# Two attentions whose first pair is loaded a phase earlier, and a third gate/up chunk with its work in another order

## The chip, the cores and the metric

The kernel runs on one core of one Trainium2 chip. A core has TensorE (matmuls; PE in the rows, with PEld for its weight loads), VectorE (DVE), ScalarE (ACT), GpSimd (POOL) and SyncE (SP), which here only issues transfers. The engines run their own instruction lists and meet at semaphores. The metric is the device time of one execution in microseconds (us), as the median of several runs.

## The reference

One inference step of a two-layer encoder on 1024 prompt tokens and 32 sample tokens (N = 1056 columns), D = 1024, all float32. Each layer is a mixer and a SwiGLU feed-forward part:

```python
# layer 0 mixer: sparse attention A (8 heads, top-k keys) beside a gated linear recurrence B
# layer 1 mixer: chunked attention C (16 heads, own chunk and 8 before)
logits = q @ k.T * DH ** -0.5 + bias;  p = softmax(logits);  out = p @ v
x = x + gate * (mix @ w_out)
h = modulate(x, norm_ffn)
x = x + gate2 * ((silu(h @ w_gate) * (h @ w_up)) @ w_down)      # D_FF = 2816
```

A matmul keeps float32 accuracy by splitting each operand into an upper half (fp32r) and a rest, and making three passes: upper by upper, rest by upper, upper by rest.

## The kernel before

The program is a row of phases, with a barrier of all engines between two of them: `front_phase` (projections of layer 0, the choice of the keys), `attention_phase` "pa" (A), the recurrence, `trunk_phase` 0, `attention_phase` "pc" (C), `trunk_phase` 1. There is no scheduler: each engine's list is written out by hand, and instructions wait on semaphores.

**The end of the front phase and of a trunk phase.** TensorE makes the last projections, ScalarE copies each to a stage and stores it to z (q and k by feature) or zt (v by token). VectorE chooses keys at the front's end and SyncE stores that mask.

**An attention phase.** Heads go in pairs g, each over 8 row tiles, unit u = (g, i). `loads(g)` on SyncE issues q, k, bias and v of a pair, two pairs ahead in two buffers; `loads(0)` and `loads(1)` are the first things in the phase. For a unit TensorE makes the scores (L2284) once q and k are in; in A GpSimd first adds bias and mask (L2255), in C it masks two corners of the bias once a pair (L2249, L2250); VectorE adds the result to the scores (L2420); ScalarE takes the exponentials (L2523); TensorE turns them (L2297) and, three units behind the scores, multiplies by v (L2312).

**The gate/up part of a trunk phase.** There are KF = 22 chunks of 128 features. The first two (f = 0, 1, "the pair") are made plainly, in four rounds of products (`pair_products`, phases 0 to 3: M1, M2 for the left half of the columns, B12, M3 for the right), each round of four: f = 0 gate, f = 0 up, f = 1 gate, f = 1 up. A product is 24 matmuls of 264 columns. From the third chunk on (f = 2, weights of unit `SEVEN`) a chunk takes seven products of a fast 2x2 scheme, in the order M1, M2, M6, M5, M7, M3, M4 (`up_products`). Its inputs for M6, M5, M7, M4 are differences of quarters `full[0]` to `full[3]` of the activations:

- ScalarE shifts the quarters (`shift_tile`, L843), 4 tiles each;
- GpSimd makes the differences in `full[0]`, `full[1]`, `full[3]` (L584, L588, L591), VectorE then the one in `full[2]` (L1332);
- ScalarE casts each to its upper half (`upper`, L867), VectorE subtracts for the rest (`lower`, L1135), in the order M6, M5, M7, M4.

In between stand the results of the pair: `pair_silu(f, right)` on ScalarE (L871) reads the gate product out of PSUM, `pair_product(f, right)` on VectorE (L1142) multiplies by the up product, `pair_store` on ScalarE's queue stores it. A PSUM bank is free only after that, so TensorE waits: in `pair_products` phase 2 for `pair_gate[f]` >= 1 and `pair_value[f]` >= 1, in `up_products(2)` before M1, M2, M6 and M5 for `pair_gate[0]`, `pair_value[0]`, `pair_gate[1]`, `pair_value[1]` >= 2. Before M7 it waits for ScalarE's copy of M1 (`keep_m1`, L900), before M3 for VectorE's first sum of the chunk (`sum_gate_left`, L1153).

The weights of a chunk are split into a ring of six slots: an upper half (cast on GpSimd, L550, or on ScalarE, L889) and a rest (GpSimd, L552); four combinations of the quarters of the weights (L561 to L567, `combine`) are on GpSimd too. `by_act` says which casts are ScalarE's: all of the chunks from `SEVEN` on, but not the first six slots of `SEVEN` itself.

## Time and profile before

| | |
|---|---|
| median of 3 runs | 3113.55 us (3110.88 to 3113.63) |
| the profiled execution, its own time | 3111.68 us |
| its span, first to last instruction | 3109.8 us |
| TensorE busy | 2917.9 us (94%) |
| VectorE, ScalarE, GpSimd busy | 1653.1, 951.2, 1321.6 us |
| mean granted clock of TensorE | 0.971 |
| phase starts: A, C | 579.96, 2006.14 us |

The granted clock is a share of full speed: 1.00 is 2.4 GHz, 0.50 is 1.2 GHz. A row of a timeline gives start, duration, engine and line; a bracket at its end gives how long the engine stood idle before it and what released it. SPq and ACTq are the queues that issue transfers.

### The profile page before, as it was taken

What the parts mean: (1) busy time and instruction counts of PE and PEld (TensorE: products, weight loads), DVE (VectorE), ACT (ScalarE), POOL (GpSimd) and SP (SyncE); (2) the same over time, 40 slices, a digit from 0 to 9 for tenths busy, and PEclk for the clock granted to TensorE, in tenths of its full rate; (3) what the DMA queues carried; (4) which work ended last, traced back from release to release, by engine and by line L of the source; (5) the groups of instructions that cost most, each with busy time, mean ns of one, the idle gap of its engine ahead of it and who ended that gap; (6) DMA issues with size and microseconds to landing.
All of it is one profiled execution on the core that took longest, in us unless ns stands there. A gap on an engine that the chain in (4) does not pass through costs nothing. (4 is left out here: it accounts for less than half of the span.)

```text
span 3109.8 us, 60214 instructions
## 1 busy us (share of the span) xinstructions
PE 2917.9 (94%) x25097; PEld 2716.4 (87%) x25097; DVE 1653.1 (53%) x2959; ACT 951.2 (31%) x1984; POOL 1321.6 (42%) x1082
## 2 busy tenths in 40 slices
PE   7999999886789899999999999899889999999998
PEld 5859999664679899999999999766689999999998
DVE  6399999564646644445346400055536644444345
ACT  3341211354433433332101311165524333332001
POOL 2112212373533877776334222100114877775334
PEclk8999999998889999999999999999989999999999
DMA  5816763633241122223321232352121122224222
GB/s 211 256 61 228 235 212 106 180 108 110 99 164 55 49 83 83 82 70 133 102 83 62 81 103 74 95 191 86 64 85 45 66 83 80 71 78 153 83 74 72
DMA packets 160465, 338.82 MB, mean 109 GB/s; under 512 B 21033, under 2 KB 94529, under 8 KB 152193
## 3 DMA queue, kind: packets, MB, share of 16 engines
q1 hardware_dynamic: 119856, 281.64, 27.0%
q10 hardware_dynamic: 40336, 53.31, 4.8%
q8 instruction: 200, 3.28, 0.4%
q14 instruction: 73, 0.59, 0.1%
HBM read 268.30 MB, written 79.49 MB: 112 GB/s over the span
## 5 line engine op out<-in xcount | busy, mean ns | idle before, releaser
L108 PE MATMUL tr_acc<-tr_quad_hi,ah_ring_hi 128*128 128x264 f32 x2432 | 696.3, 286 | 18.8 <-DVE tr_kept L1142 13.2
L110 PE MATMUL tr_acc<-tr_quad_hi,ah_ring_lo 128*128 128x264 f32 x2432 | 694.7, 286 | 0.0
L109 PE MATMUL tr_acc<-tr_quad_lo,ah_ring_hi 128*128 128x264 f32 x2432 | 692.4, 285 | 0.0
L552 POOL TENSOR_TENSOR ah_ring_lo<-ah_raw,ah_ring_hi 128x512 fp32r<-128x512 f32 (+1 forms) x402 | 553.9, 1383 | 183.0 <-ACT ah_ring_hi L889 169.2
L108 PEld LDWEIGHTS tr_acc<-tr_quad_hi,ah_ring_hi 128*128 128x128 f32 x2432 | 461.0, 190 | 19.7 <-DVE tr_kept L1142 13.6
L109 PEld LDWEIGHTS tr_acc<-tr_quad_lo,ah_ring_hi 128*128 128x128 f32 x2432 | 461.2, 190 | 0.1
L110 PEld LDWEIGHTS tr_acc<-tr_quad_hi,ah_ring_lo 128*128 128x128 f32 x2432 | 460.4, 189 | 0.0
L550 POOL CAST ah_ring_hi<-ah_raw 128x512 fp32r<-128x512 f32 (+1 forms) x172 | 113.4, 659 | 592.3 <-PE tr_acc L110 527.2
L108 PE MATMUL tr_acc<-tr_part_hi,ah_ring_hi 128*128 128x352 f32 x1038 | 335.5, 323 | 2.0 <-DVE tr_kept L1191 2.0
L109 PE MATMUL tr_acc<-tr_part_lo,ah_ring_hi 128*128 128x352 f32 x1038 | 332.8, 321 | 0.0
L110 PE MATMUL tr_acc<-tr_part_hi,ah_ring_lo 128*128 128x352 f32 x1038 | 332.5, 320 | 0.0
L1228 DVE SCALAR_TENSOR_TENSOR x<-tr_acc,mod,x 128x352 f32<-128x352 f32 (+2 forms) x384 | 166.8, 487 | 265.6 <-PE tr_acc L110 265.6
L2420 DVE CUSTOM_DVE_ANT_0 pc_prob<-pc_dots,pc_bias 128x640 f32<-128x640 f32 (+4 forms) x128 | 83.2, 652 | 348.0 <-POOL pc_bias L2250 268.2
L1412 DVE TENSOR_SCALAR_CACHE_REDUCE f_q<-score,choose_trial 128x384 bf16<-128x384 f32 (+6 forms) x224 | 242.1, 1146 | 1.1
L889 ACT ACTIVATE ah_ring_hi<-ah_raw 128x512 fp32r<-128x512 f32 x230 | 143.5, 626 | 248.1 <-POOL ah_raw L567 177.5
L108 PE MATMUL f_acc<-h_hi,f_w_hi 128*128 128x352 f32 x600 | 202.3, 337 | 6.8 <-DVE h_lo L2016 6.8
L108 PEld LDWEIGHTS tr_acc<-tr_part_hi,ah_ring_hi 128*128 128x128 f32 x1038 | 194.8, 188 | 2.5 <-DVE tr_kept L1191 2.4
L109 PEld LDWEIGHTS tr_acc<-tr_part_lo,ah_ring_hi 128*128 128x128 f32 x1038 | 195.0, 188 | 0.1
L110 PEld LDWEIGHTS tr_acc<-tr_part_hi,ah_ring_lo 128*128 128x128 f32 x1038 | 194.6, 187 | 0.0
L1714 POOL CAST f_w_hi<-f_raw 128x2048 fp32r<-128x2048 f32 (+1 forms) x15 | 28.4, 1895 | 389.9 <-DMA f_raw<-in_w_dram 197.4
L110 PE MATMUL f_acc<-h_hi,f_w_lo 128*128 128x352 f32 x600 | 193.6, 323 | 0.0
L109 PE MATMUL f_acc<-h_lo,f_w_hi 128*128 128x352 f32 x600 | 193.5, 322 | 0.0
(399 smaller groups left out, 6484.6 us busy)
## 6 DMA issues: line engine op xcount, KB each, us to landing
f_ada_w<-in_w_ada_dram SPq DMA_DIRECT2D x48, 1024.0 KB, 5.5
scratch_inner<-tr_kept ACTq DMA_DIRECT2D x88, 264.0 KB, 2.4
tr_staged<-scratch_inner SPq DMA_DIRECT2D x44, 528.0 KB, 4.0
ah_raw<-in_w_gate_dram SPq DMA_DIRECT2D x44, 512.0 KB, 3.5
ah_raw<-in_w_up_dram SPq DMA_DIRECT2D x44, 512.0 KB, 4.5
ah_raw<-in_w_down_dram SPq DMA_DIRECT2D x64, 256.0 KB, 3.1
f_raw<-in_w_dram SPq DMA_DIRECT2D x24, 512.0 KB, 7.4
out_z_dram<-f_stage ACTq DMA_DIRECT2D x60, 176.0 KB, 1.9
```

The lines of the kernel that those rows point to most:

```text
L108: pe.matmul(out, w_hi, hi, start=start, stop=False)
L109: pe.matmul(out, w_hi, lo, start=False, stop=False)
L110: return pe.matmul(out, w_lo, hi, start=False, stop=stop)
L550: pool.tensor_copy(hi[:, 0:width], own).then_inc(w_hi, 1)
L552: pool.tensor_tensor(lo[:, 0:width], own, hi[:, 0:width].bitcast(F32), ALU.subtract).then_inc(w_ready, 1)
L889: act.activation(slot(u, to)[0], factor_of(u, to), ACT.Copy).then_inc(act_hi, 1)
L1228: done = dve.scalar_tensor_tensor(out=x[:, k, lo:hi], in0=pair[s % 3][:, a, lo - THIRD * t:hi - THIRD * t], scalar=gate_ffn[:, k, of:of + ...
L1412: last = dve.tensor_scalar(marks[n % 2][0:p, 0:width], score[0:p, at:at + width], bound(p, j), 0.0, compare, ALU.add, accum_out=count[0:p, ...
L1714: pool.tensor_copy(w[b].hi[:, 0:n], raw[b][:, 0:n]).then_inc(w_hi, 1)
L2420: dve.tensor_tensor_reduce(prob[2 * (u % 3) + hd][:, 0:n], dots[hd][:, at_dots(u):at_dots(u) + n], add, -DH ** -0.5, 3.0e38, ALU.add, ALU. ...
```

## The change

It has two parts.

**First pair loaded early.** A class `FirstPair` holds q, k and bias of pair 0 at a place that the phase before no longer needs: in the front phase the two raw weight buffers, in trunk 0 the quarters 11 to 13 of the arena. SyncE issues the three loads there at the end of its list in the phase before (in the front ahead of the mask's store), behind waits for the last weight split and for the stores of z; it waits for their landing before the phase ends. The attention phase lays its other tiles around that place, issues only v for pair 0, and TensorE and GpSimd wait for no load at pair 0.

**Third chunk.** `pair_silu(1, 0)` moves ahead of M3's casts, `pair_silu(0, 1)` and `pair_silu(1, 1)` and both right `pair_product`s move forward; half of the differences in `full[1]` and `full[3]` go from GpSimd to VectorE; the six remaining casts of `SEVEN` go to ScalarE; GpSimd splits slot 2 of every chunk before its fourth combination, and ScalarE casts it after the third.

```diff
-        self.by_act = [SEVEN <= u < DOWN_FIRST and i >= self.slot_no[SEVEN, 6] for i, (u, n) in enumerate(self.slots)]
+        self.by_act = [SEVEN <= u < DOWN_FIRST for i, (u, n) in enumerate(self.slots)]
...
+        def differences(eng, k):
+            if k < KH // 2:
+                eng.wait_ge(combo, KH + KH // 2 + k + 1)
+            else:
+                eng.wait_ge(combo_upper, k + 1)
...
@@ trunk, SyncE
+            if ahead:
+                for r in range(3):
+                    sp.wait_ge(stored[r], 16 * 2 * 5)
+                ahead.loads(sp)
+                ahead.done(sp)
...
@@ combine(u), GpSimd
                 pool.wait_ge(combined, 4 * f + 3)
+                split(u, 2, r11)
                 pool.tensor_tensor(r12, r12, r11, ALU.subtract).then_inc(combined, 1)
...
-            for k in range(KH):
+            for k in range(KH // 2):
                 pool.wait_ge(shifted, 2 * KH + k + 1)
                 pool.wait_ge(combo, k + 1)
                 pool.tensor_tensor(full[1][:, k], full[3][:, k], full[1][:, k], ALU.subtract).then_inc(combo, 1)
-            for k in range(KH):
+            for k in range(KH // 2):
                 pool.wait_ge(combo, KH + k + 1)
                 pool.tensor_tensor(full[3][:, k], full[3][:, k], full[0][:, k], ALU.subtract).then_inc(combo, 1)
...
@@ cast, ScalarE
-                    act.wait_ge(combined, 4 * (u - SEVEN) + 4)
+                    act.wait_ge(combined, 4 * (u - SEVEN) + (3 if to == 2 else 4))
...
@@ the third chunk, ScalarE
             pair_silu(0, 0)
+            pair_silu(1, 0)
             for k in range(KH):
                 upper(M3, k)
...
+            pair_store(1, 0)
+            pair_silu(0, 1)
+            cast_slot(plan.slot_no[SEVEN, 0])
+            cast_slot(plan.slot_no[SEVEN, 1])
             for k in range(KH):
                 upper(M6, k)
-            pair_store(1, 0)
             for k in range(KH):
                 upper(M5, k)
-            pair_silu(0, 1)
+            pair_store(0, 1)
+            pair_silu(1, 1)
+            for n in range(2, 6):
+                cast_slot(plan.slot_no[SEVEN, n])
...
@@ the third chunk, VectorE
             pair_product(1, 0)
+            for k in range(KH // 2, KH):
+                dve.wait_ge(shifted, 2 * KH + k + 1)
+                dve.wait_ge(combo, k + 1)
+                dve.tensor_tensor(full[1][:, k], full[3][:, k], full[1][:, k], ALU.subtract).then_inc(combo_upper, 1)
+            for k in range(KH // 2, KH):
+                dve.wait_ge(combo_upper, k - KH // 2 + 1)
+                dve.tensor_tensor(full[3][:, k], full[3][:, k], full[0][:, k], ALU.subtract).then_inc(combo_upper, 1)
             for k in range(KH):
                 lower(M6, k)
+            pair_product(0, 1)
             for k in range(KH):
-                dve.wait_ge(combo, 2 * KH + k + 1)
+                differences(dve, k)
                 dve.wait_ge(shifted, 3 * KH + k + 1)
                 dve.tensor_tensor(full[2][:, k], full[2][:, k], full[3][:, k], ALU.subtract).then_inc(combo4, 1)
+            pair_product(1, 1)
             for k in range(KH):
                 lower(M5, k)
-            pair_product(0, 1)
             for k in range(KH):
                 lower(M7, k)
-            pair_product(1, 1)
...
@@ the front phase, SyncE
+            sp.wait_ge(lines_out, 48)
+            sp.wait_ge(w_ready, len(units))
+            projected = store_no[plan.last_step[len(units) - 3]] + 1
+            for r in range(3):
+                sp.wait_ge(stored[r], 16 * len(range(r, projected, 3)))
+            ahead.loads(sp)
             store_mask(sp)
-            sp.wait_ge(lines_out, 48)
+            ahead.done(sp)
...
+class FirstPair:
+    def loads(self, sp):
+        q, k, bias = self.sources
+        sp.dma_start(self.bias[:], bias).then_inc(self.landed, 16)
+        sp.dma_start(self.q[:], q).then_inc(self.landed, 16)
+        sp.dma_start(self.k[:], k).then_inc(self.landed, 16)
+    def done(self, sp):
+        sp.wait_ge(self.landed, 48)
...
@@ attention, SyncE, loads(g); the waits of GpSimd and TensorE likewise
-                sp.dma_start(q[b][:], z[q0 + g][:, 0:T]).then_inc(qk_in[b], 16)
-                sp.dma_start(k[b][:], z[k0 + g][:, 0:T]).then_inc(qk_in[b], 16)
+                if g:
+                    sp.dma_start(q[b][:], z[q0 + g][:, 0:T]).then_inc(qk_in[b], 16)
+                    sp.dma_start(k[b][:], z[k0 + g][:, 0:T]).then_inc(qk_in[b], 16)
```

How instructions stand on the engines is seen in the orders of the two programs (names with numbers are tiles: before, `tr_full_11354` to `tr_full_11357` are `full[0]` to `full[3]`, `tr_kept_11394` and `tr_kept_11396` the right values of the pair, `tr_kept_11397` the left value of f = 1; after, the same tiles are `tr_full_11361` to `tr_full_11364`, `tr_kept_11401`, `tr_kept_11403` and `tr_kept_11404`).

ScalarE at the third chunk of trunk 0, before, from the last shift:

```order
L843 ACTIVATE tr_full_11356<-tr_full_11356,mod 128x528 x4
L867 ACTIVATE tr_quad_hi<-tr_full_11357 128x528 x4
L876 DMA scratch_inner<-tr_kept_11397 128x528
L867 ACTIVATE tr_quad_hi<-tr_full_11354 128x528 x4
L871 ACTIVATE tr_kept_11394<-tr_acc 128x528
L867 ACTIVATE tr_quad_hi<-tr_full_11355 128x528 x4
L876 DMA scratch_inner<-tr_kept_11394 128x528
L871 ACTIVATE tr_kept_11396<-tr_acc 128x528
L867 ACTIVATE tr_quad_hi<-tr_full_11356 128x528 x4
L876 DMA scratch_inner<-tr_kept_11396 128x528
```

And in the changed kernel, from the same shift:

```order
L860 ACTIVATE tr_full_11363<-tr_full_11363,mod 128x528 x4
L896 DMA scratch_inner<-tr_kept_11404 128x528
L891 ACTIVATE tr_kept_11401<-tr_acc 128x528
L911 ACTIVATE ah_ring_hi<-ah_raw_9100 128x512 x2
L887 ACTIVATE tr_quad_hi<-tr_full_11364 128x528 x4
L887 ACTIVATE tr_quad_hi<-tr_full_11361 128x528 x4
L896 DMA scratch_inner<-tr_kept_11401 128x528
L891 ACTIVATE tr_kept_11403<-tr_acc 128x528
L911 ACTIVATE ah_ring_hi<-ah_raw_9100 128x512
L911 ACTIVATE ah_ring_hi<-tr_w_sum_11398 128x512
L911 ACTIVATE ah_ring_hi<-ah_raw_9100 128x512 x2
L887 ACTIVATE tr_quad_hi<-tr_full_11362 128x528 x4
```

Both right SiLUs now stand ahead of M7's casts, the first ahead of M6's too, and six weight casts are new.

VectorE at the same place, before, from the left value product of f = 1:

```order
L1142 TENSOR_TENSOR tr_kept_11397<-tr_kept_11397,tr_acc 128x528
L1135 TENSOR_TENSOR tr_quad_lo<-tr_full_11357,tr_quad_hi 128x528 x4
L1332 TENSOR_TENSOR tr_full_11356<-tr_full_11356,tr_full_11357 128x528 x4
L1135 TENSOR_TENSOR tr_quad_lo<-tr_full_11354,tr_quad_hi 128x528 x4
L1142 TENSOR_TENSOR tr_kept_11394<-tr_kept_11394,tr_acc 128x528
L1135 TENSOR_TENSOR tr_quad_lo<-tr_full_11355,tr_quad_hi 128x528 x4
L1142 TENSOR_TENSOR tr_kept_11396<-tr_kept_11396,tr_acc 128x528
L1135 TENSOR_TENSOR tr_quad_lo<-tr_full_11356,tr_quad_hi 128x528 x4
L1153 TENSOR_TENSOR tr_kept_11397<-tr_kept_11393,tr_acc 128x528
```

And in the changed kernel:

```order
L1168 TENSOR_TENSOR tr_kept_11404<-tr_kept_11404,tr_acc 128x528
L1356 TENSOR_TENSOR tr_full_11362<-tr_full_11364,tr_full_11362 128x528 x2
L1359 TENSOR_TENSOR tr_full_11364<-tr_full_11364,tr_full_11361 128x528 x2
L1161 TENSOR_TENSOR tr_quad_lo<-tr_full_11364,tr_quad_hi 128x528 x4
L1168 TENSOR_TENSOR tr_kept_11401<-tr_kept_11401,tr_acc 128x528
L1366 TENSOR_TENSOR tr_full_11363<-tr_full_11363,tr_full_11364 128x528 x4
L1168 TENSOR_TENSOR tr_kept_11403<-tr_kept_11403,tr_acc 128x528
L1161 TENSOR_TENSOR tr_quad_lo<-tr_full_11361,tr_quad_hi 128x528 x4
L1161 TENSOR_TENSOR tr_quad_lo<-tr_full_11362,tr_quad_hi 128x528 x4
L1161 TENSOR_TENSOR tr_quad_lo<-tr_full_11363,tr_quad_hi 128x528 x4
L1179 TENSOR_TENSOR tr_kept_11404<-tr_kept_11400,tr_acc 128x528
```

Four differences are new on VectorE, the right value product of f = 0 stands after four operations of M6 instead of after twelve, that of f = 1 after eight instead of sixteen.

SyncE's queue at the border of the front phase and attention A, before:

```order
L1612 DMA f_raw<-in_wt_dram 128x4x256 x4
L1469 DMA scratch_mask_s<-score 32x2080
L87 UNCONDITIONAL_BRANCH
L2161 UNCONDITIONAL_BRANCH
L2167 DMA pa_q<-out_z_dram 128x1024
L2168 DMA pa_k<-out_z_dram 128x1024
L2171 DMA pa_bias<-scratch_skew_a 128x2x1024
L2174 DMA pa_v<-out_zt_dram 128x8x128
L2167 DMA pa_q<-out_z_dram 128x1024
L2168 DMA pa_k<-out_z_dram 128x1024
```

And in the changed kernel:

```order
L1648 DMA f_raw<-in_wt_dram 128x4x256 x4
L2125 DMA pa_bias_53<-scratch_skew_a 128x2x1024
L2126 DMA pa_q_54<-out_z_dram 128x1024
L2127 DMA pa_k_55<-out_z_dram 128x1024
L1502 DMA scratch_mask_s<-score 32x2080
L88 UNCONDITIONAL_BRANCH
L2232 UNCONDITIONAL_BRANCH
L2247 DMA pa_v<-out_zt_dram 128x8x128
L2239 DMA pa_q<-out_z_dram 128x1024
L2240 DMA pa_k<-out_z_dram 128x1024
```

Bias, q and k of pair 0 went from behind the border to ahead of the mask's store; v is now the first load of the phase. At the border of trunk 0 and C the same three stand last in the trunk.

## Rows read from the trace of the kernel before

**Rows 1.** TensorE's waits, whole span: line, releaser: us in total, times, longest.
```profile
PE pa_dots L2284 <- DMA pa_k<-out_z_dram: 8.4, 1, 8.4
PE pc_dots L2284 <- DMA pc_k<-out_z_dram: 9.0, 1, 9.0
```

**Rows 2.** Timeline, start of attention A: start us, duration us, engine, line, operation.
```profile
579.96 0.37 SPq L2167 DMA_DIRECT2D pa_q<-out_z_dram  x1
...
587.74 5.37 POOL L2255 TENSOR_TENSOR pa_extra<-pa_bias,score 128x128 f32<-128x128 f32 x7 [7.32 <-DMA pa_bias<-scratch_skew_a]
...
588.35 0.29 DVE L2420 CUSTOM_DVE_ANT_0 pa_prob<-pa_dots,pa_extra 128x128 f32<-128x128 f32 x1 [19.92 <-POOL pa_extra L2255]
...
594.35 0.70 PE L2312 MATMUL pa_out<-pa_probT,pa_v 128*64 128x128 f32 x4
```

**Rows 3.** Tile pa_v, 570 to 700 us: issue to landing of its four loads.
```profile
DMA to landing us min/median/max: 3.9/8.3/13.5
```

**Rows 4.** Timeline, start of attention C.
```profile
2006.14 0.34 SPq L2167 DMA_DIRECT2D pc_q<-out_z_dram  x1
...
2013.07 0.20 POOL L2249 MEMSET pc_bias<- 64x128 f32 x1 [6.25 <-DMA pc_bias<-scratch_skew_c]
...
2013.67 0.29 DVE L2420 CUSTOM_DVE_ANT_0 pc_prob<-pc_dots,pc_bias 128x128 f32<-128x128 f32 x1 [268.16 <-POOL pc_bias L2250]
```

**Rows 5.** Timeline of SyncE's queue, 500 to 579 us, all of it.
```profile
567.67 0.34 SPq L1469 DMA_DIRECT2D scratch_mask_s<-score  x1
```

**Rows 6.** Windows: busy us (x) of PE, PEld, DVE, ACT, POOL; granted clock; DMA.
```profile
584.00:586.00 2.00, 0.95 (x6) 0.93 (x8) 0.00 (x0) 0.00 (x0) 0.00 (x0) 0.50 1.04 426
1046.00:1048.00 2.00, 1.40 (x6) 1.41 (x7) 2.00 (x3) 1.70 (x4) 2.00 (x2) 0.50 0.29 113
1052.00:1054.00 2.00, 2.00 (x17) 2.00 (x16) 2.00 (x3) 1.13 (x2) 1.92 (x3) 0.89 0.35 135
1100.00:1150.00 50.00, 50.00 (x414) 50.00 (x413) 26.65 (x25) 15.98 (x27) 38.89 (x29) 1.00 0.19 65
```

**Rows 7.** Timeline of TensorE, 1014 to 2434 us: its stops at the third chunk.
```profile
1018.62 0.59 PE L108 MATMUL tr_acc<-tr_quad_hi,ah_ring_hi 128*128 128x264 f32 x1 [2.85 <-ACT tr_kept L871]
...
1046.60 0.59 PE L108 MATMUL tr_acc<-tr_quad_hi,ah_ring_hi 128*128 128x264 f32 x1 [5.90 <-DVE tr_kept L1142]
...
2401.74 0.39 PE L108 MATMUL tr_acc<-tr_quad_hi,ah_ring_hi 128*128 128x264 f32 x1 [2.77 <-ACT tr_kept L871]
...
2429.76 0.59 PE L108 MATMUL tr_acc<-tr_quad_hi,ah_ring_hi 128*128 128x264 f32 x1 [7.27 <-DVE tr_kept L1142]
```

**Rows 8.** Timeline of ScalarE, 990 to 1060 us.
```profile
1018.46 5.87 ACT L843 ACTIVATE tr_full<-tr_full,mod 128x496 f32<-128x496 f32 x12
...
1034.74 0.59 ACT L871 ACTIVATE tr_kept<-tr_acc 128x528 f32<-128x528 f32 x1
...
1052.47 0.61 ACT L900 ACTIVATE tr_kept<-tr_acc 128x528 f32<-128x528 f32 x1 [2.78 <-PE tr_acc L110]
```

**Rows 9.** Timeline of GpSimd, 990 to 1090 us.
```profile
1015.71 5.10 POOL L584 TENSOR_TENSOR tr_full<-tr_full,tr_full 128x528 f32<-128x528 f32 x4 [25.90 <-ACT tr_full L843]
...
1025.89 6.12 POOL L591 TENSOR_TENSOR tr_full<-tr_full,tr_full 128x528 f32<-128x528 f32 x4
...
1086.00 1.29 POOL L552 TENSOR_TENSOR ah_ring_lo<-ah_raw,ah_ring_hi 128x512 fp32r<-128x512 f32 x1 [0.87 <-ACT ah_ring_hi L889]
```

**Rows 10.** Timeline of VectorE, 990 to 1060 us.
```profile
1027.94 1.14 DVE L1135 TENSOR_TENSOR tr_quad_lo<-tr_full,tr_quad_hi 128x528 fp32r<-128x528 f32 x1 [8.57 <-ACT tr_quad_hi L867]
...
1045.85 0.69 DVE L1142 TENSOR_TENSOR tr_kept<-tr_kept,tr_acc 128x528 f32<-128x528 f32 x1
...
1057.48 0.69 DVE L1153 TENSOR_TENSOR tr_kept<-tr_kept,tr_acc 128x528 f32<-128x528 f32 x1
```

**Rows 11.** Lines L1332 and L1135: ns of one, min/median/max.
```profile
L1332 DVE TENSOR_TENSOR tr_full<-tr_full,tr_full x8: 1108/1797/1810, 1033.5 to 2421.2; 128x528 f32<-128x528 f32 x8
L1135 DVE TENSOR_TENSOR tr_quad_lo<-tr_full,tr_quad_hi x4: 884/1368/1604, 1027.9 to 1032.7; 128x528 fp32r<-128x528 f32 x4
```

107 lines of the change are left out of this document (67 added, 40 removed).

## Prediction

> **What bounds the kernel now.** I read the windows first. In 1100 to 1150 us, the middle of the gate/up chunks, TensorE is busy 50.00 of 50 us at granted clock 1.00, while GpSimd has 38.89 and VectorE 26.65 [rows 6]: TensorE's queue is the bound there, and time is only to be had where it stops. The list of TensorE's waits for transfers shows two such stops, 8.4 us at the start of attention A and 9.0 us at the start of C [rows 1]; its timeline shows four at the third chunk, 2.85 and 5.90 us in trunk 0, 2.77 and 7.27 us in trunk 1 [rows 7]. The change aims at these six. The windows show a second price of a stop: after the one that ends at 1046.60 the clock stands at 0.50, and is 0.89 over 1052 to 1054, so it is back at about 1052.4 [rows 6]. A spell of 5.8 us at half speed loses 2.9 us.
>
> **First pair early, attention A.** The phase starts at 579.96, its first real step is VectorE's at 588.35, which waits for GpSimd's sum at 587.74, which waits 7.32 us for the bias [rows 2]. With bias, q and k in place GpSimd begins after its two short memsets: the sum was ready to go at 587.74 - 7.32 = 580.42, so VectorE's first step comes at 588.35 - 7.32 = 581.03. TensorE's scores need some 0.6 us from 579.96 and are no later. Gain 7.3 us. **What is late next:** v of pair 0, used first at 594.35 [rows 2], now 587.0. It was issued fourth and is now issued first, at 580.0; landings of this tile took 3.9, 8.3 in the median and 13.5 us at most [rows 3]. The 3.9 and the 8.3 give 583.9 and 588.3, the 13.5 gives 593.5; with nothing queued ahead of it I take the low half, 584 to 587, and a loss of nothing to 0.1: 7.2 us stay. The second pair is needed eight units later and issued a little earlier than before.
>
> **Attention C.** The same: start 2006.14, the mask on the bias at 2013.07 after 6.25 us of waiting for it, VectorE at 2013.67 [rows 4]. That makes 6.25 us, and the three loads that are no longer ahead of v's spare the queue 0.1: 6.4 us, from a start at 2007.3.
>
> **What the early loads cost.** In the front phase SyncE's queue issues nothing between 500 and 579 us but the mask's store at 567.67 [rows 5]. The last weight split ends long before that, so the three loads go out in the idle part, some 40 us ahead of the end, and the 13.5 us of the slowest landing seen fits three times. Without that cover they would cost what they cost now. In the trunk they follow the last weights and wait for z stores made long ago. I charge nothing for both, and up to 1 us in the range.
>
> **Third chunk, what moves.** One product is 24 matmuls; 50.00/414 us each [rows 6] gives 2.90 us. All in trunk 0's times:
> - *First stop.* TensorE stopped at 1018.62 - 2.85 = 1015.77 for the SiLU of f = 1 [rows 7], which stood behind M3's casts and four shifts. It now follows the SiLU of f = 0 and is done by about 1008.5; the value product beside it is VectorE's at 1015.7. The stop goes. Six products (the rest of phase 2, phase 3) then end at 1015.77 + 6 x 2.90 = 1033.2, M1 of f = 2 at 1036.1, M2 could follow at once.
> - *Differences.* GpSimd makes the first four from 1015.71 in 5.10 us, and four more, beside VectorE, in 6.12 [rows 9]. Now it has four left after 1020.8 where it had eight: at 1.28 to 1.53 each they end at 1025.9 to 1027.0. VectorE does its four from 1020.6, at 0.88 alone to 1.80 beside GpSimd [rows 11], by 1024.1 to 1027.8. ScalarE reaches M6's casts at 1024.5 (when phase 3's first product is done, which the SiLU of f = 0 needs) + 3 x 0.6 = 1026.3. So VectorE starts on M6's rests at about 1027.1 instead of 1027.94 [rows 10].
> - *Second stop.* TensorE waited for the value product at 1045.85 [rows 7, 10]. VectorE took 5.6 us for M6's four rests (1027.94 to 1033.5) [rows 10, 11]; the product of 0.69 us now follows them, and is done at 1033.4. M2 starts at 1036.1 without waiting, M6 at 1039.0 (its SiLU is done by 1034.6, its weights by 1037.7), and ends at 1041.9.
> - *What is late next* is VectorE's chain, which has not become shorter. After 1033.4 eight operations stand at (1045.85 - 1033.5)/8 = 1.54 us: differences to 1039.6, the second value product to 1040.3, M5's rests one by one to about 1045.8. TensorE, at M5 from 1042, goes at their pace and ends M5 near 1047.7. M7 needs ScalarE's copy of M1, which stands behind M7's and M4's casts as it did (1052.47 before) [rows 8], now about 1049.3. M3 needs the first sum, 1057.48 before [rows 10], behind eight more rests. GpSimd, rid of six casts, runs out of work near 1045; at 0.88 the eight take 7.0, and the sum is done at 1053.6. At the old rate, (1057.48 - 1046.54)/8 less the one product = 1.28, it is 1056.8.
> - *Balance.* M3 and M4 end 5.8 us after that sum: 1059.4, at the old rate 1062.6. Before, six products followed 1046.60, with the half-speed spell: 1046.60 + 17.4 + 2.9 = 1066.9. Gain 7.5 or 4.3 us. Trunk 1 differs by 1383.2: the end was 2429.76 + 20.3 = 2450.1 against 2442.6 or 2445.8, the same 7.5 or 4.3. New short stops at M5, M7 and M3 (2.7, 1.6 and 1.1 us) can bring a half-speed spell of their own. I take 6 in each trunk: near the fast end, less half a spell. Together 12.
>
> **Steady chunks.** Slot 2 is split ahead of the fourth combination; slots 3 to 6 come no earlier and no later but for a second round trip to ScalarE. Such a wait is 0.87 us [rows 9]; a chunk of 20.3 us leaves GpSimd 11.1/50 of it idle [rows 6], 4.5 us. It hides. Cost nothing; without that cover 0.87 a chunk.
>
> **A rule of the Trainium skill against this step.** L1332's operations, with two inputs in SBUF, took 1.797 us in the median beside GpSimd, where the shortest like it took 0.884 [rows 11]. "SBUF — State Buffer", Who interferes with whom, says that such a VectorE instruction and a GpSimd one that reads SBUF lock each other out for the whole instruction. By the rows' rates the shared differences end at 1027.0. Taken as a strict lock, four of 1.28 and four of 0.88 stand in one line from 1020.8 and end at 1029.4, 2.4 us later. The rows lie between: 1.54 each on VectorE over 12 us in which GpSimd too was never idle. I go by them.
>
> **The sum.** 7.2 + 6.4 + 12 = 25.6 us. 3111.68 - 25.6 = 3086.1. The profiled execution stands 1.9 us under the median of the three runs, but the lowest is below it, so I add half: 3087.
>
> **The rivals.**
> - *VectorE's chain stays the bound at its old pace and a half-speed spell comes in both trunks.* For it: the chain has 20 operations as before, and the new short stops. Per trunk 4.3 - 2.9 = 1.4. Gain 16.4: 3096.
> - *The differences take turns at SBUF.* For it the long rows of L1332. The chain is 2.4 us later in each trunk: gain 20.8: 3092. (This is the rule's case above.)
> - *The wait passes to v.* If it takes the 13.5 us in each attention, 6.4 of the gain go each time: 12.8 less, 3099. Against it: nothing is queued ahead.
> - *The clock.* At 584 to 586 it is 0.50 [rows 6], since TensorE had stopped. A stop of 3.5 us instead of 8.4 may spare one spell of 2.9 in each attention: 5.8 more, 3081.
> - *Slower.* The second round trip delays the rest of slot 3 in each of 20 chunks in two trunks, 0.87 each if GpSimd's queue has no slack: +35 against -25.6 makes 3121. It decides from the point where the idle 4.5 us of a chunk are used up; the windows speak against it.
> - *Nothing.* The engines' starts move, but another wait of the same length stands behind each: 3112.
>
> **How the numbers follow.** Forecast 0.62 (3080 to 3092 its own range), chain and clock 0.15, turns at SBUF 0.08, v 0.05, clock kept 0.04, slower 0.03, nothing 0.03. 3079 to 3096 leaves out v, slower, nothing and the tails. A measurement tells 0.2% (6.2 us) from no change. Faster by more: 0.62 + 0.15 + 0.08 + 0.05 + 0.04 = 0.94; within 0.03; slower 0.03.
>
> **What would show it.** Right: no transfer among TensorE's waits at either attention; VectorE's first step 1.1 to 1.2 us after the phase's start; the value product of f = 0 right before 1033.5 less what came off earlier, no stop of TensorE at M2; in their place short stops at M5, M7 and M3, released by VectorE and ScalarE. Wrong: a wait of TensorE for v; GpSimd named as releaser in the steady chunks; a first sum of the chunk no earlier than before by 1 us; the phase borders moved later by the early loads.

## The result, and the profile after

The changed kernel takes 3084.07 us in the median of four runs (3080.31 to 3085.46), the kernel before 3113.59 (3110.88 to 3119.29). The ratio is 0.9897 with a 95% interval of 0.988 to 0.9915: faster by 29.5 us by the medians. The forecast was 3087, with a range of 3079 to 3096. The profiled execution took 3085.13 us, its span is 3083.3, 26.5 less than before; the prediction's sum of 25.6 us was made for such a pair.

| | before | after |
|---|---|---|
| span of the profiled execution | 3109.8 | 3083.3 |
| TensorE busy | 2917.9 | 2912.0 |
| mean granted clock | 0.971 | 0.976 |
| A: start of the phase to the last value product | 145.1 | 139.0 |
| trunk 0: first to last product of the gate/up part | 470.4 | 463.5 |
| C: start of the phase to the last value product | 236.6 | 230.2 |
| trunk 1: first to last product of the gate/up part | 472.0 | 465.2 |

The last four lines are differences of the first and the last start that the views of one tile give (the value products that read v; the products that read the tile of quarters; for a phase's start SyncE's first load in it). They give 6.2 (before rounding), 6.9, 6.4 and 6.8, together 26.3 us. In this pair of profiles these four places are the whole change, and the rest of the program takes as long as before (from trunk 0's last gate/up product to the start of C, where the early loads of C are issued, 551.9 us against 552.0). Another profile of the changed kernel, after_again below, differs elsewhere by 3.4 us.

**The attentions.** The timelines of the profile after, at the start of A, against [rows 2]:

```profile
533.25 0.37 SPq L2125 DMA_DIRECT2D pa_bias<-scratch_skew_a  x1
...
534.18 0.43 SPq L2127 DMA_DIRECT2D pa_k<-out_z_dram  x1
...
580.45 0.40 SPq L2247 DMA_DIRECT2D pa_v<-out_zt_dram  x1
...
580.98 22.75 POOL L2328 TENSOR_TENSOR pa_extra<-pa_bias,score 128x128 f32<-128x128 f32 x18
...
581.59 0.29 DVE L2493 CUSTOM_DVE_ANT_0 pa_prob<-pa_dots,pa_extra 128x128 f32<-128x128 f32 x1 [13.38 <-POOL pa_extra L2328]
...
580.48 0.93 PE L2357 MATMUL pa_dots<-pa_k,pa_q 64*128 64x128 f32 x8 [3.36 <-PEq L80]
```

and of C, against [rows 4]:

```profile
1993.44 0.38 SPq L2247 DMA_DIRECT2D pc_v<-out_zt_dram  x1
...
1994.18 0.20 POOL L2322 MEMSET pc_bias<- 64x128 f32 x1
...
1994.78 0.29 DVE L2493 CUSTOM_DVE_ANT_0 pc_prob<-pc_dots,pc_bias 128x128 f32<-128x128 f32 x1 [261.67 <-POOL pc_bias L2323]
```

The three loads of A are issued at 533 us, 47 us ahead of the phase, those of C at 1890.9 to 1891.9, 101 us ahead. In the phase v is the first load, VectorE's first step comes 1.1 us after the start in A and 1.3 in C, where it was 8.4 and 7.5. TensorE waits for no transfer at either place; the 3.36 us in front of its row are the border itself.

**The third chunk.** TensorE's stops there, in trunk 0 (the first four rows) and trunk 1, against [rows 7]:

```profile
1037.26 0.36 PE L109 MATMUL tr_acc<-tr_quad_hi,ah_ring_hi 128*128 128x264 f32 x1 [0.90 <-issue]
...
1039.48 0.39 PE L109 MATMUL tr_acc<-tr_quad_hi,ah_ring_hi 128*128 128x264 f32 x1 [0.90 <-DVE tr_quad_lo L1161]
...
1047.23 0.39 PE L109 MATMUL tr_acc<-tr_quad_hi,ah_ring_hi 128*128 128x264 f32 x1 [1.01 <-DVE tr_kept L1179]
...
1062.79 0.39 PE L109 MATMUL tr_acc<-tr_quad_hi,ah_ring_hi 128*128 128x264 f32 x1 [0.72 <-DVE tr_kept L1224]
...
2412.46 0.39 PE L109 MATMUL tr_acc<-tr_quad_hi,ah_ring_hi 128*128 128x264 f32 x1 [1.27 <-ACT tr_kept L922]
...
2416.84 0.39 PE L109 MATMUL tr_acc<-tr_quad_hi,ah_ring_hi 128*128 128x264 f32 x1 [1.20 <-DVE tr_kept L1179]
```

The stops of 2.85 and 5.90 us, 2.77 and 7.27 in trunk 1, are gone. In their place are stops of about 1 us: two in M5 (0.90 each), one at M7 (1.27 in trunk 1), one at M3 (1.01 and 1.20), and one of 0.72 in the chunk behind, which the prediction's sum did not have. The first of the two in M5 names no releaser, but M5 reads the weights of slot 3, and GpSimd's rest of that slot ends at 1037.15, right before it; M5's second stop is for VectorE's rests. VectorE and GpSimd there, against [rows 9, 10]:

```profile
1014.84 2.67 DVE L1356 TENSOR_TENSOR tr_full<-tr_full,tr_full 128x528 f32<-128x528 f32 x2 [4.17 <-ACT tr_full L860]
...
1017.42 3.59 DVE L1359 TENSOR_TENSOR tr_full<-tr_full,tr_full 128x528 f32<-128x528 f32 x2
...
1021.16 6.76 DVE L1161 TENSOR_TENSOR tr_quad_lo<-tr_full,tr_quad_hi 128x528 fp32r<-128x528 f32 x4
...
1027.84 0.69 DVE L1168 TENSOR_TENSOR tr_kept<-tr_kept,tr_acc 128x528 f32<-128x528 f32 x1
...
1028.45 5.22 DVE L1366 TENSOR_TENSOR tr_full<-tr_full,tr_full 128x528 f32<-128x528 f32 x4
...
1034.21 12.35 DVE L1161 TENSOR_TENSOR tr_quad_lo<-tr_full,tr_quad_hi 128x528 fp32r<-128x528 f32 x12
...
1046.49 0.69 DVE L1179 TENSOR_TENSOR tr_kept<-tr_kept,tr_acc 128x528 f32<-128x528 f32 x1
...
1018.65 3.54 POOL L608 TENSOR_TENSOR tr_full<-tr_full,tr_full 128x528 f32<-128x528 f32 x2
...
1035.70 1.45 POOL L568 TENSOR_TENSOR ah_ring_lo<-tr_w_sum,ah_ring_hi 128x512 fp32r<-128x512 f32 x1 [0.87 <-ACT ah_ring_hi L911]
...
1048.52 3.01 POOL L568 TENSOR_TENSOR ah_ring_lo<-ah_raw,ah_ring_hi 128x512 fp32r<-128x512 f32 x2 [3.76 <-ACT ah_ring_hi L911]
```

VectorE has no gap of more than 0.2 us from 1014.84 to the first sum, which is done at 1047.18; M3 starts at 1047.23. GpSimd ends its differences at 1022.2, and stands idle for 3.76 us ahead of 1048.52. The windows, against [rows 6]:

```profile
584.00:586.00 2.00, 2.00 (x6) 0.65 (x6) 1.21 (x5) 1.59 (x6) 2.00 (x3) 0.53 1.04 414
586.00:588.00 2.00, 1.24 (x10) 0.62 (x8) 1.53 (x5) 1.36 (x4) 2.00 (x3) 1.00 1.02 403
1040.00:1042.00 2.00, 2.00 (x11) 2.00 (x10) 2.00 (x3) 2.00 (x5) 0.58 (x1) 0.50 0.35 135
1042.00:1044.00 2.00, 2.00 (x12) 1.71 (x12) 2.00 (x4) 1.31 (x3) 0.61 (x1) 0.69 0.00 0
1100.00:1150.00 50.00, 50.00 (x414) 50.00 (x413) 19.77 (x21) 15.40 (x26) 37.54 (x28) 1.00 0.26 89
```

In A the clock is back at full by 586 us. In trunk 0 a short spell at half speed follows the stops in M5; trunk 1 shows none (2402 to 2422 us at 1.00). The spell cost nothing here: from M5's start to M7's it is 5.59 us in trunk 0 (1037.26 to 1042.85) and 5.60 in trunk 1 (2406.86 to 2412.46), since M7 waits for ScalarE's copy of M1 either way, and the stop of 1.27 us of trunk 1 is what the spell fills in trunk 0. bounds_later below has the stop and not the spell in trunk 0, and the trunk takes 463.6 us, as long as here. The steady chunks are as they were: TensorE busy 50.00 of 50 us with the same 414 matmuls.

### The profile page after: what moved, and what is told of

It is laid out like the page before. It is cut to its first block and busy times, and to the rows that moved or that the text cites. A ratio compares the mean times of both kernels' runs of the same rounds, so it can differ in the third digit from the quotient of the medians.

```text
span 3083.3 us, 60268 instructions
## 1 busy us (share of the span) xinstructions
PE 2912.0 (94%) x25097; PEld 2709.4 (88%) x25097; DVE 1617.8 (52%) x2967; ACT 955.1 (31%) x1996; POOL 1300.1 (42%) x1062
## 5 line engine op out<-in xcount | busy, mean ns | idle before, releaser
L566 POOL CAST ah_ring_hi<-ah_raw 128x512 fp32r<-128x512 f32 (+1 forms) x162 | 103.9, 641 | 593.4 <-PE tr_acc L111 527.2
```

What stands on the lines that cost most here:

```text
L566: pool.tensor_copy(hi[:, 0:width], own).then_inc(w_hi, 1)
```

## The experiments

Every variant computes the whole reference. Its time is the median of four or five executions, and its ratio is taken to executions of the kernel before beside it. A single program spreads over 3 to 11 us between executions, so differences under 3 us are read from the phases of the profiles, which repeat within 0.3 us in the trunks. There is one profile behind each row. The table gives for each kernel the four stretches of the table above.

| kernel | time | ratio to before, interval | A | trunk 0 | C | trunk 1 |
|---|---|---|---|---|---|---|
| before | 3111.8 to 3113.6 | | 145.1 | 470.4 | 236.6 | 472.0 |
| changed | 3084.07 | 0.9897, 0.988 to 0.9915 | 139.0 | 463.5 | 230.2 | 465.2 |
| after_again | 3083.02 | 0.9904, 0.9888 to 0.9921 | 139.0 | 463.5 | 230.1 | 465.3 |
| early_only | 3097.71 | 0.9959, 0.9946 to 0.9972 | 141.0 | 470.6 | 230.4 | 471.7 |
| third_only | 3098.98 | 0.9955, 0.9942 to 0.9967 | 146.5 | 463.5 | 236.6 | 465.2 |
| silu_back | 3085.70 | 0.9915, 0.9902 to 0.9929 | 139.1 | 466.2 | 230.5 | 466.6 |
| value_back | 3099.95 | 0.9959, 0.9947 to 0.9972 | 137.9 | 470.9 | 230.7 | 472.5 |
| diffs_back | 3091.12 | 0.993, 0.9917 to 0.9942 | 139.4 | 466.8 | 230.3 | 468.6 |
| casts_back | 3089.46 | 0.993, 0.9917 to 0.9942 | 141.1 | 466.7 | 230.4 | 469.7 |
| split_back | 3080.71 | 0.9897, 0.9882 to 0.9912 | 138.9 | 462.2 | 229.1 | 464.0 |
| sum_first | 3086.71 | 0.9922, 0.9907 to 0.9936 | 137.4 | 466.1 | 230.5 | 465.2 |
| sums_first | 3083.01 | 0.9903, 0.9888 to 0.9918 | 137.9 | 462.3 | 229.2 | 464.1 |
| bounds_later | 3081.02 | 0.9895, 0.988 to 0.9909 | 135.2 | 463.6 | 230.2 | 465.2 |
| best | 3080.57 | 0.9889, 0.9874 to 0.9904 | 135.8 | 462.3 | 230.7 | 464.1 |

### The two parts alone

**early_only** is the kernel before with all hunks of the early loads and none of the third chunk; **third_only** is the reverse.

> The kernel before with the early loads of both attentions alone; the third chunk as before. In the profile of the changed kernel the steps of A stand 7.3 us earlier from the fourth unit on and 5.7 us earlier after the stop of TensorE near 664 us, behind which the clock is low there and was not before; C gains 6.6. Theory: the two parts of the change add up, this one gives 12.3 (A 5.7, C 6.6) and the time is 3101. Rival 1: the low clock near 664 is chance and does not come with the early loads; then A keeps 7.3 and the time is 3099.7. Rival 2: the later start of A (0.48 us) comes with the wait at the front's end; then A starts 0.5 us later here too, otherwise not.

> The kernel before with the third chunk's part alone, no early loads. Theory: the parts add up; each trunk gives 6.7 to 6.8, 13.5 together, and the time is 3100. The stops of TensorE at the third chunk are the four short ones of the changed kernel (0.90, 0.90, 1.01 and, a chunk later, 0.72). Rival: one part takes from the other (the queue of SyncE, the clock at the phase borders); then the gains of the two alone sum to more or less than 29 by over 3 us.

In the trunks and C the parts add up: early_only has the trunks of before (within 0.3 us) and the changed kernel's C; third_only has the changed kernel's trunks to the tenth and the C of before. In A one profile of each does not show it: early_only gives 4.1 us there and third_only is 1.4 longer than before, against 6.2 for both. Spells at half speed go with that: third_only has one behind the stop near 664 us, which the profile of before has not, and early_only has a longer one at the start of A than the changed kernel (0.72 against 0.91 in the mean clock of 577 to 595 us). By the medians early_only gives 14.1 us and third_only 12.8 (3111.76 less each), 26.9 together against 29.5 and 30.2 for both, the measurements of the changed kernel; that is within their spread. Of the rivals, the first is right in its cause: the low clock near 664 us does not come with the early loads, for third_only, which has none, shows it too. It fell in early_only as well, so the 7.3 us of A that this rival promised are not seen. The second rival is out: A starts at 579.2 in early_only, no later than before (579.96), against 580.45 with the change and 578.5 to 582.7 in the others. That start moves from execution to execution.

### The first stop: silu_back

```diff
-            pair_silu(1, 0)
             for k in range(KH):
                 upper(M3, k)
             for k in range(KH):
                 shift_tile(1, k)
             pair_store(0, 0)
+            pair_silu(1, 0)
```

> The changed kernel with the second left SiLU back behind M3's casts and the first four shifts. Theory: VectorE's chain of work from 1014.84 to 1047.18 has no gap and sets when M5 and M3 can run; TensorE's stop of 2.8 us at the third product of phase 2 comes back in each trunk, but the stops at M5 (0.90, 0.90), M7 and M3 (1.01) shrink by as much, M3 starts at the same time, and the time stays within 1 us of the changed kernel's, 3084. Rival: each stop counts by itself; then 2.8 in each trunk come on top, 5.7 in all: 3090, or 3096 with a spell at half speed behind each stop.

Neither theory holds. The stop is back in both trunks (2.84 and 2.76 us), and they grow by 2.7 and 1.4 us: half of the stop is absorbed, and in trunk 0 a spell at half speed comes on top (0.51 and 0.64 over 1010 to 1014 us), which trunk 1 does not have. VectorE's chain, which was to hide the stop, has moved with it:

```profile
1042.93 0.39 PE L109 MATMUL tr_acc<-tr_quad_hi,ah_ring_hi 128*128 128x264 f32 x1 [1.27 <-ACT tr_kept L922]
...
1020.77 0.61 ACT L891 ACTIVATE tr_kept<-tr_acc 128x528 f32<-128x528 f32 x1 [4.78 <-PE tr_acc L111]
...
1022.99 6.08 DVE L1161 TENSOR_TENSOR tr_quad_lo<-tr_full,tr_quad_hi 128x528 fp32r<-128x528 f32 x4 [3.40 <-ACT tr_quad_hi L887]
```

The stop makes phase 3 late. ScalarE waits 4.78 us for phase 3's first product, with M6's casts behind that SiLU, and VectorE waits 3.40 us for those casts, a gap that the changed kernel does not have. So a stop of TensorE travels through ScalarE's in-order list to the chain that the later products wait for. What absorbs the other half are the stops in M5, which are gone but for 0.27 us in trunk 0 and 0.16 in trunk 1.

### The second stop: value_back

```diff
             for k in range(KH):
                 lower(M6, k)
-            pair_product(0, 1)
...
-            pair_product(1, 1)
             for k in range(KH):
                 lower(M5, k)
+            pair_product(0, 1)
             for k in range(KH):
                 lower(M7, k)
+            pair_product(1, 1)
```

> The changed kernel with both right value products of VectorE back behind the rests of M5 and of M7. Theory: the place of this one product is what the second stop hung on. The rests of M5 would end near 1037.3, the product at 1038, TensorE is there at 1030.4: a stop of 7.6 us at M2 and a spell at half speed (2.9), then six products of 2.90 to 1058.3 instead of 1053.0, less the stop of 0.72 in the chunk behind: 4.6 to 5.3 in each trunk, 9 to 11 in all: 3094. Rival: what gave the gain is the shorter work of GpSimd and the faster rests, and the place of the product is worth under 1 us a trunk: 3086 at most.

```profile
1033.57 0.59 PE L109 MATMUL tr_acc<-tr_quad_hi,ah_ring_hi 128*128 128x264 f32 x1 [5.26 <-DVE tr_kept L1168]
...
1045.27 0.59 PE L109 MATMUL tr_acc<-tr_quad_hi,ah_ring_hi 128*128 128x264 f32 x1 [4.04 <-DVE tr_kept L1168]
...
1030.35 2.55 DVE L1161 TENSOR_TENSOR tr_quad_lo<-tr_full,tr_quad_hi 128x528 fp32r<-128x528 f32 x4
```

The place of two products of 0.69 us is worth the whole gain of the trunks: 7.4 and 7.3 us, 15.9 in the medians. The first stop is shorter than expected (5.26 for 7.6), but I had left out the second: M5 needs the other bank, which f = 1's product frees only behind M7's rests, another 4.04 us. Each of the two stops is followed by half speed (0.50 to 0.62 in trunk 0), in both trunks. So the trunks lose 14.7 us where I expected 9 to 11. The last row is of use below: four rests of M5 in 2.55 us, 0.64 each.

### Who makes what: diffs_back and casts_back

diffs_back gives GpSimd all eight differences again:

```diff
-            for k in range(KH // 2):
+            for k in range(KH):
                 pool.wait_ge(shifted, 2 * KH + k + 1)
...
-            for k in range(KH // 2):
+            for k in range(KH):
                 pool.wait_ge(combo, KH + k + 1)
...
-            for k in range(KH // 2, KH):
-                dve.wait_ge(shifted, 2 * KH + k + 1)
-                dve.wait_ge(combo, k + 1)
-                dve.tensor_tensor(full[1][:, k], full[3][:, k], full[1][:, k], ALU.subtract).then_inc(combo_upper, 1)
-            for k in range(KH // 2, KH):
-                dve.wait_ge(combo_upper, k - KH // 2 + 1)
-                dve.tensor_tensor(full[3][:, k], full[3][:, k], full[0][:, k], ALU.subtract).then_inc(combo_upper, 1)
```

> The changed kernel with all eight differences in the second and fourth quarter back on GpSimd. Theory (VectorE's chain and GpSimd's weights take turns as the bound): GpSimd ends its differences at 1026.3 instead of 1022.15, so the weights of M6 come 4.2 us later, at 1037.3, and TensorE stops about 4 us at M6; but M3 waits for VectorE's sum anyway, which comes at 1046.5 at the latest, so most of it is absorbed: 0 to 1 us a trunk, and up to 2.9 more where a spell at half speed follows. 3084 to 3090, I take 3087. Rival: the differences on VectorE are worth the 4.2 us of each trunk: 3092. Rival 2: they take turns with GpSimd's at the memory and are worth nothing; the stop at M6 does not come: 3083.

casts_back gives GpSimd the six casts:

```diff
-        self.by_act = [SEVEN <= u < DOWN_FIRST for i, (u, n) in enumerate(self.slots)]
+        self.by_act = [SEVEN <= u < DOWN_FIRST and i >= self.slot_no[SEVEN, 6] for i, (u, n) in enumerate(self.slots)]
...
-            cast_slot(plan.slot_no[SEVEN, 0])
-            cast_slot(plan.slot_no[SEVEN, 1])
...
-            for n in range(2, 6):
-                cast_slot(plan.slot_no[SEVEN, n])
```

> The changed kernel with the six casts of the third chunk's first slots back on GpSimd. Theory: GpSimd makes them in 0.7 to 0.9 us each and spares the 0.87 us of the round trips; slot 2 comes at 1034.9 instead of 1033.1 (a stop of 1.6 at M6), slot 3 at 1039 (M5 a further 1 to 2 late), which the stops at M7 and M3 absorb, unless VectorE's rests, with GpSimd busy beside them, go back from 1.03 to 1.3 us each: then M3 waits 3 us more. 0 to 3 us a trunk: 3084 to 3090, I take 3087. Rival: ScalarE, not GpSimd, is short (M7 waits for its copy of M1 behind the casts); then it gets faster: 3082.

Both cost more than the top of what I gave them in a trunk: 3.3 and 3.4 us, 3.2 and 4.5. The timelines of diffs_back:

```profile
1033.06 0.56 PE L109 MATMUL tr_acc<-tr_quad_hi,ah_ring_hi 128*128 128x264 f32 x1 [2.91 <-issue]
...
1018.21 6.33 DVE L1157 TENSOR_TENSOR tr_quad_lo<-tr_full,tr_quad_hi 128x528 fp32r<-128x528 f32 x4 [11.67 <-ACT tr_quad_hi L883]
...
1031.93 13.86 DVE L1157 TENSOR_TENSOR tr_quad_lo<-tr_full,tr_quad_hi 128x528 fp32r<-128x528 f32 x12
```

and of casts_back:

```profile
1048.73 0.39 PE L109 MATMUL tr_acc<-tr_quad_hi,ah_ring_hi 128*128 128x264 f32 x1 [3.16 <-DVE tr_kept L1175]
...
1032.79 15.27 DVE L1157 TENSOR_TENSOR tr_quad_lo<-tr_full,tr_quad_hi 128x528 fp32r<-128x528 f32 x12
```

In diffs_back the weights of M6 came late as reckoned (a stop of 2.91 us, in trunk 0 with 8 us at a clock of 0.55 to 0.59 around and behind it; 2.87 in trunk 1 without). The spell adds nothing there: both trunks lose the same. What failed is that M3 would wait no longer: counted from the trunk's first gate/up product, VectorE reaches its last twelve rests 1.8 us later than in the changed kernel, and they took 13.86 us where the changed kernel has 12.35; M3 waits 1.65 us for the sum. In casts_back VectorE reaches the twelve on time (0.2 us earlier), but they took 15.27 us, with GpSimd busy beside them up to 1046.25, and M3 waits 3.16 us. Behind that stop half speed follows, for longer in trunk 1, where M3 and M4 take 8.7 us against 7.4 in trunk 0, which is why the second loses more (4.5 against 3.2). The rests' pace, and with it M3, goes with how busy GpSimd is beside them.

### The second round trip: split_back

```diff
                 pool.wait_ge(combined, 4 * f + 3)
-                split(u, 2, r11)
                 pool.tensor_tensor(r12, r12, r11, ALU.subtract).then_inc(combined, 1)
...
-                for n in range(3, 7):
+                for n in range(2, 7):
                     split(u, n, factor_of(u, n))
...
-                    act.wait_ge(combined, 4 * (u - SEVEN) + (3 if to == 2 else 4))
+                    act.wait_ge(combined, 4 * (u - SEVEN) + 4)
```

> The changed kernel with slot 2 split behind the fourth combination in every chunk, as before. Theory: in the steady chunks GpSimd has 4.5 us of slack and the order costs and gives nothing; in the third chunk slot 2 comes 1.76 us later, which the stops behind it absorb: 3084 to 3086. Rival: the second round trip to ScalarE costs something in every chunk that the step forward has hidden; without it the time falls, by up to 0.87 in each of 40 chunks. Rival 2: the step forward gives something in every chunk; without it the time rises by over 3 us.

```profile
1034.31 0.36 PE L109 MATMUL tr_acc<-tr_quad_hi,ah_ring_hi 128*128 128x264 f32 x1 [1.55 <-issue]
...
1043.34 0.39 PE L109 MATMUL tr_acc<-tr_quad_hi,ah_ring_hi 128*128 128x264 f32 x1 [1.28 <-ACT tr_kept L921]
...
1033.61 11.25 DVE L1160 TENSOR_TENSOR tr_quad_lo<-tr_full,tr_quad_hi 128x528 fp32r<-128x528 f32 x12
...
1043.89 2.13 POOL L568 TENSOR_TENSOR ah_ring_lo<-ah_raw,ah_ring_hi 128x512 fp32r<-128x512 f32 x1 [4.54 <-ACT ah_ring_hi L910]
```

In the steady chunks there is nothing, as forecast: ScalarE's copies of M5 follow each other by 20.4 us in both programs. But the third chunk is 1.3 and 1.2 us shorter without this step of the change. M6 waits 1.55 us for its weights and M5 once, 1.07 for its rests, where M5 waited twice 0.90; the stop at M7 is 1.28 us in both trunks; GpSimd goes to ScalarE and back once less (0.87 us), is done earlier and idle for 4.54 us, and VectorE's twelve rests take 11.25 instead of 12.35 us. M3 and the chunk behind then wait for nothing, and the clock stays at 1.00. So by the profiles one step of the change costs 2.5 us. The times don't tell: the ratio to the kernel before is 0.9897, against 0.9897 and 0.9904 for the changed kernel.

### Moving the sums: sum_first and sums_first

sum_first moves one sum and the copy of M1:

```diff
             pair_store(1, 1)
+            keep_m1(2)
             for k in range(KH):
                 upper(M4, k)
...
+            sum_gate_left(2)
             for k in range(KH):
                 lower(M4, k)
```

> The changed kernel with the third chunk's copy of M1 on ScalarE ahead of M4's casts and its first sum on VectorE ahead of M4's rests: a version that may beat both. Theory: M3 and, behind it, GpSimd hang on that sum: GpSimd stands idle 3.76 us ahead of 1048.52 for a cast that stands behind the SiLU of that sum on ScalarE, and the stop of 0.72 at 1062.79 in the next chunk comes from there. With the sum at about 1042.8 the stops at M7 (0.4), M3 (1.0) and in the next chunk (0.7) go: 2.1 to 2.8 in each trunk, 3079. Rival: M4 then waits for its rests, or the next chunk's stop grows by as much: no change, 3084.

```profile
1045.79 0.59 PE L109 MATMUL tr_acc<-tr_quad_hi,ah_ring_hi 128*128 128x264 f32 x1 [3.00 <-DVE tr_kept L1188]
...
1038.27 6.84 DVE L1163 TENSOR_TENSOR tr_quad_lo<-tr_full,tr_quad_hi 128x528 fp32r<-128x528 f32 x4
```

The stops at M7 and M3 went, and one of 3.00 us came at M4 in both trunks, for the second sum (L1188), which now stood behind four rests of 1.7 us each. In trunk 1 the one makes up for the others to the tenth; in trunk 0 half speed follows (0.62 and 0.53 over 1044 to 1052 us), and it is 2.6 us longer. The next version moves both sums, the copy further forward, and takes split_back's order:

```diff
+            keep_m1(2)
             for k in range(KH):
                 upper(M7, k)
...
+            sum_gate_left(2)
+            sum_u2(2)
             for k in range(KH):
                 lower(M4, k)
```

> The changed kernel with slot 2 split behind the fourth combination as before, ScalarE's copy of M1 ahead of M7's casts, and VectorE's first two sums of the third chunk ahead of M4's rests: the one step of the change that the runs showed to cost something taken back, and the two waits behind M5 taken away. Theory: the split gives 1.3 us in each trunk (462.2 and 464.0); the copy takes away the stop of 1.28 at M7, the sums the half us that M3 would then wait, and M4 finds its sum and its rests, which the version with one sum moved did not: 460.9 and 462.7, 5 us less than the changed kernel in all, 3079 against 3084. Rival: M6's stop of 1.55 at its weights grows, or M5 waits longer for its rests: then 462 and 464, 3081.5.

```profile
1051.23 0.40 PE L109 MATMUL tr_acc<-tr_quad_hi,ah_ring_hi 128*128 128x264 f32 x1 [1.05 <-DVE tr_quad_lo L1162]
...
1044.52 6.65 DVE L1162 TENSOR_TENSOR tr_quad_lo<-tr_full,tr_quad_hi 128x528 fp32r<-128x528 f32 x4
...
1044.18 4.73 POOL L568 TENSOR_TENSOR ah_ring_lo<-ah_raw,ah_ring_hi 128x512 fp32r<-128x512 f32 x3 [4.04 <-ACT ah_ring_hi L910]
```

Its trunks are split_back's, 462.3 and 464.1, and its time 3083.01 against the 3079 expected: the sums gave nothing. M7 and M3 wait no more, but M4 waits 1.05 us for its own rests, the first of the three rows. The other two show why. The earlier sum frees the SiLU on ScalarE and the cast behind it, so GpSimd takes up the next chunk's weights at 1044.18, and from there VectorE's four rests of M4 take 6.65 us; with GpSimd idle four took 2.55.

### A stop in A: bounds_later, best, after_again

```diff
-                elif head and s == U // 2 + 4:
+                elif head and s == U // 2 + 9:
                     head.bounds(dve)
                     head.gains(dve)
```

> The changed kernel with four small operations for the recurrence (2.6 us of VectorE in A, one of 1.80 us on 128x4 beside a GpSimd operation of 2.08) five units later, among short units. Theory: TensorE's stop of 2.93 us near 664 comes from them, and the half clock behind it, where it falls, from the stop. Among short units VectorE has idle time: the stop shrinks to 1.1, A takes 137.3 less 1.8 = 135.5 us in every execution, 1.8 to 3.4 less than the changed kernel: 3081 to 3082. Rival: the stop only moves with them; then A takes as long as now.

> The version with both sums first and slot 2 behind the fourth combination, and the recurrence's small operations five units later besides: a version that may beat both. Theory: the two add up, 5 and 1.8 to 3.4: 3076. Rival: A's part gives nothing: 3079.

> The changed kernel itself once more, as the measure for the three others on the same chip. Trunk 0 from its first product to the last of the gate/up part took 463.5 us and trunk 1 465.2 in its profile (470.4 and 472.0 before), and attention A 138.9 from its first score to the last value product with a stretch at half clock behind the stop near 664 us that the runs so far show in four of eight programs of the changed kind. Theory: the trunks and C repeat within 0.3 us, A is 1.6 us shorter if that stretch is not there, and what remains of the spread of 5 us between executions lies in the front phase and the recurrence.

In the changed kernel, where these operations stand, the timelines of GpSimd, VectorE and TensorE and a window:

```profile
658.98 2.08 POOL L2328 TENSOR_TENSOR pa_extra<-pa_bias,score 128x896 f32<-128x896 f32 x1
...
659.07 0.18 DVE L2733 RECIPROCAL hg_lbt<-hg_lbt 128x4 f32<-128x4 f32 x1
...
659.28 1.80 DVE L2735 TENSOR_TENSOR hg_lbt<-hg_lbt 128x4 f32<-128x4 f32 x1
...
664.36 2.72 PE L2357 MATMUL pa_dots<-pa_k,pa_q 64*128 64x512 f32 x6 [2.93 <-DVE pa_least L2493]
```

```profile
664.00:666.00 2.00, 1.64 (x4) 0.84 (x6) 0.31 (x2) 1.03 (x2) 2.00 (x2) 0.59 0.00 0
```

and the same operation in bounds_later:

```profile
682.00 0.16 DVE L2735 TENSOR_TENSOR hg_lbt<-hg_lbt 128x4 f32<-128x4 f32 x1
...
663.04 1.77 PE L2357 MATMUL pa_dots<-pa_k,pa_q 64*128 64x512 f32 x8 [0.78 <-DVE pa_least L2493]
```

L2735 works on 128x4 elements. Beside GpSimd's sum it took 1.80 us and ended with it (658.98 + 2.08 = 661.06, 659.28 + 1.80 = 661.08); among short units, with GpSimd idle, 0.16. The RECIPROCAL between them, with one input, took 0.18 us beside the same GpSimd operation. The stop of 2.93 us shrinks to 0.78. (The edit also moves `head.gains`, 0.7 us of six small operations, which stand behind these.) A takes 135.2 us, and 135.8 in best, where I had 135.5; in the changed kernel it took 139.0 with a spell at half speed behind the stop, and in other versions with early loads 137.4 to 137.9 without. By the medians bounds_later is 2.0 us and best 2.5 us under after_again, in the direction of the four stretches' sum of 3.7 and 5.0 us less, but within the spread. best is the fastest of all by its ratio, 0.9889, but its interval overlaps the changed kernel's, and it stays short of the 3076 expected.

after_again repeats trunks and attentions within 0.1 us. Its span is 3.4 us shorter than the first profile's all the same, and the difference lies in the recurrence, between A's last value product and trunk 0's first product: 157.9 for 161.3 us. Over all profiles this stretch takes 155.9 to 162.8 us, with no relation to what a kernel changes. This part of the expectation held; A did not shrink, since the half clock was there again.

## Why the prediction was right

The time was in the range and 3 us from the forecast; by the profiled executions, 26.5 us gained against 25.6. The total is closer than its parts: A gave 1.0 us less than its term, the trunks 1.7 more.

- **A, 7.2: 6.2 measured.** The step itself gave what was forecast: VectorE's first step is 7.2 us nearer the phase's start (8.39 against 1.14), and behind the first units, with the clock back 9 us sooner, 7.8. Then 1.6 are lost at half speed behind a stop near 664 us that is as long before (2.95) but cost no clock there. The stop was followed by half speed in eight of twelve profiles, third_only among them, and not in before, value_back, sum_first and sums_first: it goes with the execution, not with the early loads.
- **v is no wait.** Its loads landed in 3.9 to 9.8 us, that of pair 0 in 4.1, at 584.6; the first use is at 586.8, and no wait of TensorE names it. (The 3099 of that rival should be 3100 by its own 12.8 us.) The rival on v is out.
- **C, 6.4: 6.4.** VectorE's first step is 6.2 us nearer the phase's start (7.53 against 1.34).
- **The early loads cost nothing.** A's start moved by +0.5 us with the change and -0.7 with the loads alone, within the spread of the others, and the stretch from trunk 0's last gate/up product to C is 551.7 to 552.0 us in all profiles, with early loads and without.
- **The first stop goes, and its removal counts,** at half its length: silu_back prices it at 1.4 us, and 2.7 where half speed follows. The prediction let its removal carry through phase 3; my later theory, that VectorE's chain hides it, fell.
- **The second stop, value first.** The place of VectorE's product is what it hung on (value_back, 7.4 us a trunk).
- **The new stops at M5, M7 and M3**, put at 2.7, 1.6 and 1.1 us, are 1.7 to 1.8, up to 1.3, and 1.0 to 1.2. They are released by VectorE and ScalarE as said, but for the first half of M5's, which waits for GpSimd's rest of the weights; the prediction had only VectorE's chain there.
- **The first sum** was put at 1053.6. The changed trunk runs 5.7 us ahead of the old times (GpSimd's first difference 1010.01 for 1015.71), so its 1047.18 is 1052.9. That this is near is in part luck, since two errors cancelled: M6's rests took 1.69 us each, not 1.40, and the four differences behind them 1.30 each (5.22 together), not 1.54. The last twelve took 12.35 us where the prediction had 12.5 (four at 1.37, eight at 0.88).
- **The balance, 6 a trunk: 6.9 and 6.8.** At the end of M4 the gain was 7.9 us in trunk 0 (the next chunk's first product starts at 1053.17 + 5.7 = 1058.9, against 1066.8) and 7.7 in trunk 1, near the fast end of 7.5. What came off again, 1.0 and 0.9, is a term that I had not seen, the stop of 0.72 us in the next chunk. Its chain starts with the late sum: GpSimd waits for a cast behind that sum's SiLU, its next operations come late, and with them a SiLU on ScalarE and the two operations of VectorE that TensorE waits for. The half a spell that the prediction took off did not come as a cost: the spell of trunk 0 is hidden at M7, and trunk 1 has none. It was about the right size for the wrong item, which is luck.
- **Turns at the memory.** The rival's price was 2.4 us a trunk, for differences that end at 1029.4 instead of 1027.0; they ended at 1022.2 + 5.7 = 1027.9, between the two. It did not decide, but VectorE's pace goes with it throughout, and the last section has its numbers. The rule that the prediction weighed, the Trainium skill's in "SBUF — State Buffer", Who interferes with whom, agrees with the row of L2735, whose end is GpSimd's end within 0.02 us.
- **The second round trip** costs nothing in a steady chunk, and 1.2 to 1.3 us in the third, where GpSimd has no slack. I had counted its slack only where the windows show it, in the steady chunks.
- **The clock in the attentions.** The spells were shorter but not spared: over 577 to 595 us the mean clock was 0.62 before and 0.91 in the changed kernel, 0.72 to 0.91 in the other kernels with early loads. Of those that also have half speed behind the stop near 664 us, A took 141.0 and 141.1 us with 0.72 and 138.9 to 139.4 with 0.81 or 0.91. So it may be worth 2 us; no run sets the clock apart from the execution.

What stays open: why a given stop of TensorE is followed by half speed in one execution or trunk and not in another (the Trainium skill, "TensorE: Matmul & The Clock Gate", Part 1, says that one kernel meets the change of clock at other points from run to run, which these profiles agree with and don't explain), and what makes the recurrence take 156 to 163 us. Neither was tried.
